# x in eight pieces, a first unit by halves, products of ones ahead of it, and transfers that wait for the landing two units back

## The chip, the core and the metric

The kernel runs on one core of a Trainium2 chip. The metric is the device time of one execution in microseconds (us). The engines that matter here: TensorE (PE in the profile, with PEld for its weight loads), VectorE (DVE), ScalarE (ACT) and the sync engine SP, which issues nearly all transfers from HBM. ACT can issue transfers too, on a queue of its own (ACTq in the profile; SP's is SPq). A semaphore orders work between engines: an instruction waits until a count is reached, and each engine works in program order, so what waits holds up all that stands behind it on its engine.

## The reference, cut to what matters

Two transformer blocks one after the other, on 256 tokens of 2048 features, in float32. Only the first step of the first block is touched here:

```
def first_block(x, mem, w_in, ...):
    h = rms_norm(x, g_mix[l])                       # x: [1, 256, 2048]
    qa, ka, va, qb, kb, vb, qc, kc, vc = jnp.split(h @ w_in[l], cuts, axis=-1)   # w_in: [2048, 6144]
    ... three attentions, w_out, cross attention, a gated feed-forward
def second_block(x, p, positions, ...):
    ... feed-forward, attention and recurrence, feed-forward, a gated output
```

What follows that first product reads the same numbers as before; some 600 MB of weights go through the chip once in all, and w_in is the first of them.

## The kernel before, in words

Activations lie transposed: features on the 128 partitions, in 16 chunks of 128 features, and 256 tokens along the free axis. x is X, 128 x 16 x 256.

Weights come in *units*: 256 rows by 512 columns (512 KB), as two chunks of 128 rows. Unit u lands in slot u % 4 of `raw`. Every float32 product is done as three products of a reduced-precision kind: a number is split into a high part and the rest. For a unit, ACT copies raw into `wh` with rounding (`split`, L1174), DVE subtracts and writes the rest into `wl` (`split`, L1761), and then PE multiplies high by high and rest, and rest by high (L675, L677, L680). The unit's counters are `raw_full` (landed), `hi_done`, `lo_done` and `units_used` (PE has read it). SP may load a unit into a slot when `lo_done` says that the unit four before it has been split, so from unit 4 on it waits there.

x takes the same two parts. For each chunk c ACT writes gain times x (L1314, counter `xs_hi`), and DVE the rest (L1989, `xs_lo`); the normalisation's factor, one over the root of the mean square, is multiplied in after the product, so the products can begin before it is known. PE needs xs_lo for the two chunks of unit u and lo_done for the unit.

The product with w_in goes by blocks of 512 columns, each of 8 units (8 x 2 chunks = all 2048 rows): units 0 to 7 are the first block, 8 to 15 the second. In the first block ACT and DVE prepare x beside the weights: two chunks of x, one unit, two chunks, one unit. Around it stands more:

- After unit 3 PE makes a small product for the position biases from three tables (L697, waits for `tab_loaded`). DVE adds to it, behind unit 7's split (L1995, `rt_sb`), and ACT stores the sum to HBM (L1317) before it goes on to unit 8.
- Then ACT takes turns between the splits of units 8 to 11 and the squares of x by four chunks (L1306); DVE takes turns between the rest of the splits and the sums of these squares (L1908, L1895, L1896). Between them DVE makes a small lambda (L2005 to L2008, from `lam`), and collects the first block's product (L1775) behind ACT's copy of it (L1192).
- PE sums the squares over partitions with a matrix of ones (`late_stat`, L634) at a fixed place in its order: after unit 10, the third of the second block. It waits there for `colsum_ready`, which DVE's L1896 sets.

At the program's start SP issues x in four pieces of four chunks (512 KB each), each ahead of one of units 0 to 3. ACT issues seven transfers of its own: all gain vectors (`vec`, 264 KB), a gate bias, the identity, the three tables and lambda's four vectors spread over all partitions. The first use of ACT's function table loads it (ACT_TABLE_LOAD).

Of the kernel before, what the change touches and what calls it, by code (L numbers as in the profile page):

```python
# [22 lines left out]
F32 = mybir.dt.float32  # L23
F32R = mybir.dt.float32r
I32 = mybir.dt.int32
ALU = mybir.AluOpType
ACT = mybir.ActivationFunctionType
AX_X = mybir.AxisListType.X

P = 128  # L30
# [176 lines left out]
def program(nc, a, out):  # L207
    with ExitStack() as ctx:
# [40 lines left out]
        def sem(name):  # L249
            return ctx.enter_context(nc.semaphore(name))  # L250
# [6 lines left out]
        x_in = [sem(f"x_in{i}") for i in range(4)]  # L257
# [208 lines left out]
        def _(sp):  # L466
            def load_x(g):
                sp.dma_start(X[:, 4 * g:4 * g + 4, :], a["x"].rearrange("(c p) t -> p c t", p=P)[:, 4 * g:4 * g + 4, :])\
                  .then_inc(x_in[g], 16)

# [8 lines left out]
            def stream(name, col, weight, rows=256, width=NB):  # L479
                ph = PH[name]  # L480

                def first_pair():

                    for u in range(2 * ph["upc"]):
                        src = weight(u % 2)[u // 2 * rows:(u // 2 + 1) * rows, bass.ds(col(u % 2, 0), width)]
                        load(ph["u0"] + u, 0, src.rearrange("(k p) n -> p k n", p=P))

                def block(c, i):
                    if name in PAIRED and isinstance(i, int) and c < 2:
                        if c == 0:  # L490
                            first_pair()
                        return
                    for u in range(ph["upc"]):
                        w, first = weight(c), col(c, i)
                        if name == "w_in" and c == 0 and u < 4:
                            load_x(u)
                        src = w[u * rows:(u + 1) * rows, bass.ds(first, width)]
                        load(ph["u0"] + c * ph["upc"] + u, i * (2 * ph["upc"]),
                             src.rearrange("(k p) n -> p k n", p=P))
                run_blocks(sp, ph, block, peel=1 if name == "w_in" or name in PAIRED else 0)  # L500
# [65 lines left out]
        def _(pe):  # L566
# [69 lines left out]
            def gemm(name, opr, ready, tiles=4, norm=None, after=None, cross=False, half=None, post=False):  # L636
# [9 lines left out]
                def block(c, i):  # L646
# [8 lines left out]
                    for v in range(2 * ph["upc"] if paired else ph["upc"]):  # L655
# [11 lines left out]
                        pe.wait_ge(lo_done, i * (2 * ph["upc"]) + (n + 1))  # L667
# [21 lines left out]
                        else:  # L689
                            for k in range(chunks):  # L690
                                if singly:
                                    pe.wait_ge(xs_lo, half + k + 1)
                                mm = chunk(k, range(tiles))
# [20 lines left out]
            gemm("w_in", *from_op(XS["mix"]), norm="mix")  # L714
# [443 lines left out]
        def _(act):  # L1158
            act.dma_start(vec[:, :], a["vec"]).then_inc(vec_loaded, 16)
            act.dma_start(SM[0:24, 56:57], a["gate_b"]).then_inc(gb_loaded, 16)  # L1160
            act.dma_start(ident[:, :], a["cst"][:, 0:P]).then_inc(cst_loaded, 16)
            act.dma_start(HF[0:32, 0:16], a["table"]).then_inc(tab_loaded, 16)
            act.dma_start(HF[0:32, 512:1024], a["onehot"]).then_inc(tab_loaded, 16)
            act.dma_start(HF[0:16, 1024:1536], a["diag"]).then_inc(tab_loaded, 16)
            act.dma_start(T2[:, 0, :], a["lam"].rearrange("a n -> (a n)").partition_broadcast(P))\
               .then_inc(lam_loaded, 16)
# [143 lines left out]
            for u in range(DC // 2):  # L1310
                if u % 2 == 0:
                    act.wait_ge(x_in[u // 2], 16)
                for c in (2 * u, 2 * u + 1):
                    act.activation(OPR[:, c, 0, :], X[:, c, :], ACT.Copy, scale=v("g_mix", c)).then_inc(xs_hi, 1)  # L1314
                split(u, 0)
# [434 lines left out]
        def _(dve):  # L1750
# [232 lines left out]
            dve.wait_ge(vec_loaded, 16)  # L1983
            for u in range(DC // 2):
                if u % 2 == 0:
                    dve.wait_ge(x_in[u // 2], 16)
# [4 lines left out]
                split(u, 0)  # L1991
# [751 lines left out]
```

## Time and profile before

| | us |
|---|---|
| median of 3 runs | 3259.98 (3259.1 to 3260.28) |
| profiled execution | 3258.8 |
| its span, first to last instruction | 3256.7 |
| PE busy in it | 3225.5 (99%) |
| DVE busy | 2100.2 (64%) |
| ACT busy | 1586.5 (49%) |
| first product of PE starts at | 10.09 |

The profiled execution is one run; its time is 2.1 us more than its span, and 1.2 us under the median of the runs. All times below are counted from the span's start. In a timeline the first number is an instruction's start and the second its length; lengths on PE overlap, so that what a product costs is read from start to start.

### The profile page before, as it was taken

Reading aid. Unit: us, or ns where it says so; the run is one execution under the profiler, and the core shown is the slowest. Engines: PE = TensorE matmul, PEld = TensorE weight load, DVE = VectorE, ACT = ScalarE, POOL = GpSimd, SP = SyncE. Lnnn points to the kernel's source line nnn. Section 1 sums busy time; section 2 is a strip of 40 time slices with the busy share of each in tenths; the row PEclk is TensorE's granted clock in tenths of the full one; section 3 lists DMA queues with packets and bytes.
Section 4 is the critical chain, followed back from the end, with each engine's and each line's share of the span. In section 5 each row is a group of like instructions: output and inputs, shape, how many; then the busy total and the mean of one; then the engine's idle time right before and its main releaser. Section 6 shows DMA issues by size and latency. Waiting matters only on the chain.

```text
span 3256.7 us, 51030 instructions
## 1 busy us (share of the span) xinstructions
PE 3225.5 (99%) x19828; PEld 2867.5 (88%) x19828; DVE 2100.2 (64%) x2266; ACT 1586.5 (49%) x1897; POOL 88.5 (3%) x36
## 2 busy tenths in 40 slices
PE   8999999999999999999999999999999999999997
PEld 7999988888888888888888888999988888888886
DVE  6666777766665556655555456867986656554568
ACT  5445555555454435544444344555744444444354
POOL 0000200000000100000000010000010000000101
PEclk9999999999999999999999999999999999999999
DMA  8555655666666565666565555654556565566654
GB/s 265 176 156 158 193 176 173 190 186 189 189 183 193 187 192 162 189 192 187 180 199 188 188 188 168 208 180 130 171 166 188 181 197 185 184 194 192 190 176 135
DMA packets 322172, 596.30 MB, mean 183 GB/s; under 512 B 18309, under 2 KB 42277, under 8 KB 322021
## 3 DMA queue, kind: packets, MB, share of 16 engines
q1 hardware_dynamic: 313872, 587.27, 58.7%
q10 hardware_dynamic: 8148, 6.90, 0.7%
q8 instruction: 109, 1.79, 0.2%
q14 instruction: 43, 0.34, 0.0%
HBM read 591.97 MB, written 2.13 MB: 182 GB/s over the span
## 4 chain that ended last, share of the span: by engine, by line
PE 96%; DVE 2%; ACT 1%; issue 0%; POOL 0%; DMA 0%; ACTq 0%; DVEq 0%; POOLq 0%
PE acc L675 26%; PE acc L677 25%; PE acc L680 24%; PE acc L728 5%; PE acc L731 5%; PE acc L730 5%; DVE WHL L1761 0%; PE acc L959 0%; PE acc L581 0%; PE acc L755 0%; PE acc L920 0%; PE acc L921 0%; PE acc L842 0%; PE acc L840 0%; PE acc L841 0%
## 5 line engine op out<-in xcount | busy, mean ns | idle before, releaser
L1761 DVE TENSOR_TENSOR WHL<-raw,WHL 128x1024 fp32r<-128x1024 f32 x1112 | 1384.7, 1256 | 977.0 <-ACT WHL L1174 975.9
L1174 ACT ACTIVATE WHL<-raw 128x1024 fp32r<-128x1024 f32 x1112 | 1164.3, 1057 | 1260.0 <-PE acc L680 1019.7
L677 PEld LDWEIGHTS acc<-OPR,WHL 128*128 128x128 f32 x4928 | 926.7, 188 | 204.1
L675 PE MATMUL acc<-OPR,WHL 128*128 128x512 f32 x2624 | 1026.0, 397 | 11.5 <-DVE WHL L1761 10.3
L677 PE MATMUL acc<-OPR,WHL 128*128 128x256 f32 x4928 | 996.6, 278 | 0.0
L680 PE MATMUL acc<-OPR,WHL 128*128 128x512 f32 x2304 | 911.7, 396 | 0.0
L675 PEld LDWEIGHTS acc<-OPR,WHL 128*128 128x128 f32 x2624 | 498.1, 190 | 29.9 <-issue 13.5
L677 PEld LDWEIGHTS acc<-HR,WHL 128*128 128x128 f32 x2184 | 410.3, 188 | 94.5
L675 PE MATMUL acc<-HR,WHL 128*128 128x512 f32 x1120 | 440.3, 395 | 0.0
L677 PE MATMUL acc<-HR,WHL 128*128 128x256 f32 x2184 | 433.9, 278 | 0.0
L680 PEld LDWEIGHTS acc<-OPR,WHL 128*128 128x128 f32 x2304 | 431.9, 187 | 0.0
L680 PE MATMUL acc<-HR,WHL 128*128 128x512 f32 x1064 | 420.9, 396 | 0.0
L728 PE MATMUL acc<-OPR,WHL 128*128 128x256 f32 x1216 | 349.5, 287 | 0.0
L731 PE MATMUL acc<-OPR,WHL 128*128 128x256 f32 x1216 | 343.9, 283 | 0.0
L730 PE MATMUL acc<-OPR,WHL 128*128 128x256 f32 x1216 | 343.9, 283 | 0.0
L728 PEld LDWEIGHTS acc<-OPR,WHL 128*128 128x128 f32 x1216 | 232.7, 191 | 5.4 <-issue 3.6
L730 PEld LDWEIGHTS acc<-OPR,WHL 128*128 128x128 f32 x1216 | 232.8, 191 | 1.6 <-issue 0.7
L731 PEld LDWEIGHTS acc<-OPR,WHL 128*128 128x128 f32 x1216 | 232.7, 191 | 0.0
L675 PEld LDWEIGHTS acc<-HR,WHL 128*128 128x128 f32 x1120 | 212.5, 190 | 2.6
L680 PEld LDWEIGHTS acc<-HR,WHL 128*128 128x128 f32 x1064 | 199.4, 187 | 0.0
L1192 ACT ACTIVATE T<-acc 128x1024 f32<-128x1024 f32 x91 | 92.0, 1011 | 18.2 <-PE acc L680 15.6
L1495 ACT ACTIVATE HR<-T 128x1024 f32 (+1 forms) x33 | 35.0, 1061 | 127.3 <-DVE T L2242 122.5
(374 smaller groups left out, 2093.7 us busy)
## 6 DMA issues: line engine op xcount, KB each, us to landing
raw<-in_w_up SPq DMA_DIRECT2D x176, 512.0 KB, 4.5
raw<-in_ff_w_gate SPq DMA_DIRECT2D x176, 512.0 KB, 3.8
raw<-in_ff_w_up SPq DMA_DIRECT2D x176, 512.0 KB, 4.4
raw<-in_ff_w_down SPq DMA_DIRECT2D x176, 512.0 KB, 4.1
raw<-in_w_in SPq DMA_DIRECT2D x170, 512.0 KB, 4.2
raw<-in_w_down SPq DMA_DIRECT2D x88, 512.0 KB, 4.3
raw<-in_w_out SPq DMA_DIRECT2D x64, 512.0 KB, 4.1
raw<-in_w_ple_gate SPq DMA_DIRECT2D x32, 512.0 KB, 4.9
```

The lines of the kernel that those rows point to most:

```text
L675: pe.matmul(acc[:, b + t, :], wh[:, s, col:col + P], x, start=first, stop=False)
L677: mm = pe.matmul(acc[:, b + t, 0:T], wl[:, s, col:col + P], x[:, 0, :], start=False, stop=last and t % 2 == 0)
L680: mm = pe.matmul(acc[:, b + t, :], wh[:, s, col:col + P], x, start=False, stop=last)
L728: pe.matmul(dst, w_hi, ks[k][:, 0, :], start=first and k == 0 and t % 2 == 0, stop=False, skip_group_check=True)
L730: pe.matmul(dst, w_hi, ks[k][:, 1, :], start=False, stop=False, skip_group_check=True)
L731: mm = pe.matmul(dst, w_lo, ks[k][:, 0, :], start=False, stop=last and k == 1, skip_group_check=True)
L1174: act.activation(wh[:, s, :], raw[:, s, :], ACT.Copy).then_inc(hi_done, 1)
L1192: act.activation(T1[:, 0:tiles, :], acc[:, b:b + tiles, T:2 * T], ACT.Copy).then_inc(t1_full, 1)
L1495: act.activation(HR[:, bass.ds(i * 4 + 4 * j, 4), 0, :], T2[:, :, :], ACT.Copy).then_inc(hid_hi, 1)
L1761: dve.tensor_tensor(wl[:, s, :], raw[:, s, :], wh[:, s, :].bitcast(F32), ALU.subtract)\
```

## The change

- x comes in eight pieces of two chunks (256 KB), one ahead of each of units 0 to 7.
- From unit 2 on SP issues x's piece and the unit only when the unit two back has landed (a wait on `raw_full`). The wait on `lo_done` from unit 4 on stays.
- Unit 0 comes as two transfers of 128 rows (256 KB each); ACT and DVE split each half by itself, between the chunks of x, and PE begins with the first half as soon as that and chunk 0 are there (`half=XS["mix"]` makes it wait for each chunk).
- ACT issues only the first 16 columns of `vec` (the gain of x, 8 KB). The three tables move to SP, between x's piece and unit 4; the rest of `vec`, the gate bias, the identity and lambda's vectors move to SP, between x's last piece and unit 7.
- ACT makes one copy of a single column at once, so that the function table is loaded there.
- PE makes 11 products of ones (128 x 128, float32) before the first unit.

```diff
             def load_x(g):
-                sp.dma_start(X[:, 4 * g:4 * g + 4, :], a["x"].rearrange("(c p) t -> p c t", p=P)[:, 4 * g:4 * g + 4, :])\
+                sp.dma_start(X[:, 2 * g:2 * g + 2, :], a["x"].rearrange("(c p) t -> p c t", p=P)[:, 2 * g:2 * g + 2, :])\
                   .then_inc(x_in[g], 16)
+
+            def load_tables():
+                sp.dma_start(HF[0:32, 0:16], a["table"]).then_inc(tab_loaded, 16)
+                sp.dma_start(HF[0:32, 512:1024], a["onehot"]).then_inc(tab_loaded, 16)
+                sp.dma_start(HF[0:16, 1024:1536], a["diag"]).then_inc(tab_loaded, 16)
+
+            def load_constants():
+                sp.dma_start(vec[:, 16:NVEC], a["vec"][:, 16:NVEC]).then_inc(vec_loaded, 16)
+                sp.dma_start(SM[0:24, 56:57], a["gate_b"]).then_inc(gb_loaded, 16)
+                sp.dma_start(ident[:, :], a["cst"][:, 0:P]).then_inc(cst_loaded, 16)
+                sp.dma_start(T2[:, 0, :], a["lam"].rearrange("a n -> (a n)").partition_broadcast(P))\
+                  .then_inc(lam_loaded, 16)
...
-                        if name == "w_in" and c == 0 and u < 4:
+                        if name == "w_in" and c == 0:
+                            if u >= 2:
+                                sp.wait_ge(raw_full[(u - 2) % SLOTS], 16 * ((u - 2) // SLOTS + 1))
                             load_x(u)
+                            if u == 4:
+                                load_tables()
+                            if u == 7:
+                                load_constants()
+                        if name == "w_in" and c == 0 and u == 0:
+                            sp.dma_start(raw[:, 0, 0:NB], w[0:P, 0:NB]).then_inc(w_first, 16)
+                            sp.dma_start(raw[:, 0, NB:2 * NB], w[P:2 * P, 0:NB]).then_inc(raw_full[0], 16)
+                            continue
...
-                        pe.wait_ge(lo_done, i * (2 * ph["upc"]) + (n + 1))
+                        if n > 0:
+                            pe.wait_ge(lo_done, i * (2 * ph["upc"]) + (n + 1))
...
+                                if n == 0 and k == 0:
+                                    pe.wait_ge(lo_first, 1)
+                                if n == 0 and k == 1:
+                                    pe.wait_ge(lo_done, 1)
...
-            gemm("w_in", *from_op(XS["mix"]), norm="mix")
+            pe.wait_ge(ones_set, 3)
+            for _ in range(11):
+                pe.matmul(acc[:, 7, 0:P], ones[:, :], ones[:, :], start=True, stop=True)
+            gemm("w_in", *from_op(XS["mix"]), half=XS["mix"], norm="mix")
...
-            act.dma_start(vec[:, :], a["vec"]).then_inc(vec_loaded, 16)
...
+            act.dma_start(vec[:, 0:16], a["vec"][:, 0:16]).then_inc(vec_loaded, 16)
+            act.wait_ge(ones_set, 1)
+            act.activation(SM[:, 62:63], SM[:, 60:61], ACT.Copy)
...
             for u in range(DC // 2):
-                if u % 2 == 0:
-                    act.wait_ge(x_in[u // 2], 16)
+                act.wait_ge(x_in[u], 16)
                 for c in (2 * u, 2 * u + 1):
                     act.activation(OPR[:, c, 0, :], X[:, c, :], ACT.Copy, scale=v("g_mix", c)).then_inc(xs_hi, 1)
-                split(u, 0)
+                    if c == 0:
+                        act.wait_ge(w_first, 16)
+                        act.activation(wh[:, 0, 0:NB], raw[:, 0, 0:NB], ACT.Copy).then_inc(hi_first, 1)
+                    if c == 1:
+                        act.wait_ge(raw_full[0], 16)
+                        act.activation(wh[:, 0, NB:2 * NB], raw[:, 0, NB:2 * NB], ACT.Copy).then_inc(hi_done, 1)
+                if u >= 1:
+                    split(u, 0)
+            act.wait_ge(vec_loaded, 32)
             act.wait_ge(rt_sb, 1)
...
+            def lo_half(k, full, done):
+
+                dve.wait_ge(full, 1)
+                part = slice(k * NB, (k + 1) * NB)
+                dve.tensor_tensor(wl[:, 0, part], raw[:, 0, part], wh[:, 0, part].bitcast(F32), ALU.subtract)\
+                   .then_inc(done, 1)
```

DVE's loop changes as ACT's does: `lo_half` behind chunk 0 and chunk 1, `split(u, 0)` from unit 1 on, and a wait for 32 on `vec_loaded` behind the loop.

The end of SP's start, before (the fourth piece of x and all that follows it; in brackets what a row waits for):

```order
L468 DMA X<-in_x 128x4x256
L477 DMA raw<-in_w_in 128x2x512
L468 DMA X<-in_x 128x4x256
L477 DMA raw<-in_w_in 128x2x512
L477 DMA raw<-in_w_in 128x2x512 [waits lo_done] x92
```

SP now, from x's third piece to the end of the first block (`raw_full0` to `raw_full3` are the landings of units 0 to 3, and of units 4 and 5 when they are waited for again; T_58 holds lambda's vectors):

```order
L469 DMA X<-in_x 128x2x256 [waits raw_full2]
L473 DMA HF<-in_table 32x16
L474 DMA HF<-in_onehot 32x512
L475 DMA HF<-in_diag 16x512
L490 DMA raw<-in_w_in 128x2x512 [waits lo_done]
```

```order
L469 DMA X<-in_x 128x2x256 [waits raw_full1]
L478 DMA vec<-in_vec 128x513
L479 DMA SM<-in_gate_b 24x1
L480 DMA ident<-in_cst 128x128
L481 DMA T_58<-in_lam 128x256
L490 DMA raw<-in_w_in 128x2x512 [waits lo_done] x89
```

The first of the two is unit 4 with its piece of x, the second unit 7 (and the first row of all later units): three and four transfers stand ahead of these units now, behind a wait for units 2 and 5, where before all pieces of x went out without a wait.

ACT at its start, before, from its last own transfer on:

```order
L1165 DMA T_58<-in_lam 128x256
L1314 ACT_TABLE_LOAD [waits x_in0]
L1314 ACTIVATE OPR<-X,vec 128x256 [waits vec_loaded]
L1314 ACTIVATE OPR<-X,vec 128x256
L1174 ACTIVATE WHL<-raw 128x1024 [waits raw_full0]
```

and now:

```order
L1190 DMA vec<-in_vec 128x16
L1192 ACT_TABLE_LOAD
L1192 ACTIVATE SM<-SM 128x1 [waits ones_set]
L1339 ACTIVATE OPR<-X,vec 128x256 [waits x_in0,vec_loaded]
L1342 ACTIVATE WHL<-raw 128x512 [waits w_first]
L1339 ACTIVATE OPR<-X,vec 128x256
L1345 ACTIVATE WHL<-raw 128x512 [waits raw_full0]
```

The table's load no longer stands behind a wait for x, and the first half of unit 0 stands behind one chunk of x instead of the whole unit behind two. From unit 8 on the rows of ACT, DVE and PE are the same in both kernels, in the same order.

## Rows read from the trace of the kernel before

**Rows 1.** The page: the chain that ended last, by engine.
```profile
PE 96%; DVE 2%; ACT 1%; issue 0%; POOL 0%; DMA 0%; ACTq 0%; DVEq 0%; POOLq 0%
```

**Rows 2.** The chain of waits, first 60 us: start, length, what.
```profile
0.75 4.71 DMA X<-in_x
5.54 1.28 ACT L1314
6.83 0.91 ACT OPR L1314 x2
7.74 0.95 ACT WHL L1174
8.72 1.24 DVE WHL L1761
```

**Rows 3.** Timeline of PE: start, length, line, operation; in brackets idle before.
```profile
10.09 0.77 PE L675 MATMUL acc<-OPR,WHL 128*128 128x512 f32 x1 [10.09 <-DVE WHL L1761]
10.87 0.63 PE L675 MATMUL acc<-OPR,WHL 128*128 128x512 f32 x1
...
14.51 0.47 PE L675 MATMUL acc<-OPR,WHL 128*128 128x512 f32 x1
...
24.17 0.50 PE L675 MATMUL acc<-OPR,WHL 128*128 128x512 f32 x1
...
35.42 0.39 PE L675 MATMUL acc<-OPR,WHL 128*128 128x512 f32 x1
...
43.81 0.59 PE L634 MATMUL acc<-S,ones 128*128 128x256 f32 x2
...
3239.16 1.99 PE L612 MATMUL acc<-S,ones 128*128 128x256 f32 x8 [0.75 <-ACT S L1228]
```

**Rows 4.** DMA in four stretches: the last number is GB/s.
```profile
0.00:4.20 4.20, 0.00 (x0) 0.00 (x0) 0.26 (x3) 0.00 (x0) 0.20 (x4) 1.00 0.43 130
0.00:5.45 5.45, 0.00 (x0) 0.00 (x0) 0.26 (x3) 0.00 (x0) 0.20 (x4) 1.00 0.58 189
0.00:7.60 7.60, 0.00 (x0) 0.00 (x0) 0.38 (x4) 2.05 (x3) 0.20 (x4) 1.00 0.73 240
12.00:20.00 8.00, 7.97 (x43) 6.70 (x42) 5.17 (x7) 5.95 (x10) 0.00 (x0) 1.00 1.06 381
```

**Rows 5.** Timeline of DVE: the ones, units 6 and 7, and the sums of squares.
```profile
0.91 0.17 DVE L1982 MEMSET ones<- 128x128 f32 x1
...
24.66 1.22 DVE L1761 TENSOR_TENSOR WHL<-raw,WHL 128x1024 fp32r<-128x1024 f32 x1
...
26.59 1.22 DVE L1761 TENSOR_TENSOR WHL<-raw,WHL 128x1024 fp32r<-128x1024 f32 x1
...
42.27 0.69 DVE L1895 TENSOR_TENSOR S<-S 128x512 f32<-128x512 f32 x1
43.00 0.42 DVE L1896 TENSOR_TENSOR S<-S 128x256 f32<-128x256 f32 x1
```

**Rows 6.** Timeline of ACT, the splits of units 8 and 11.
```profile
28.84 1.06 ACT L1174 ACTIVATE WHL<-raw 128x1024 fp32r<-128x1024 f32 x1 [3.02 <-DVE HF L1995]
...
35.68 1.06 ACT L1174 ACTIVATE WHL<-raw 128x1024 fp32r<-128x1024 f32 x1 [0.78 <-PE acc L680]
```

**Rows 7.** Timelines of SP and ACT: transfers issued, start and length.
```profile
1.25 0.50 SPq L477 DMA_DIRECT2D raw<-in_w_in  x1
...
2.40 0.95 ACTq L1162 DMA_DIRECT2D HF<-in_table  x1
...
4.61 0.54 ACTq L1165 DMA_DIRECT2D T<-in_lam  x1
...
31.19 0.37 SPq L477 DMA_DIRECT2D raw<-in_w_in  x1
```

**Rows 8.** Issue to landing, units issued at 31.19 and 35.48, each alone.
```profile
raw<-in_w_in SPq DMA_DIRECT2D x1, 512.0 KB, 3.6
...
raw<-in_w_in SPq DMA_DIRECT2D x1, 512.0 KB, 4.8
```

More of the change, by code:

```diff
@@ L256, in program @@
         hid_hi, hid_lo = sem("hid_hi"), sem("hid_lo")
-        x_in = [sem(f"x_in{i}") for i in range(4)]
+        x_in = [sem(f"x_in{i}") for i in range(8)]
+        w_first, hi_first, lo_first = sem("w_first"), sem("hi_first"), sem("lo_first")
         out_stored, vec_loaded, cst_loaded = sem("out_stored"), sem("vec_loaded"), sem("cst_loaded")
@@ L1158, in _ @@
         def _(act):
-            act.dma_start(vec[:, :], a["vec"]).then_inc(vec_loaded, 16)
[L1160 to L1166, printed above, removed]
+            act.dma_start(vec[:, 0:16], a["vec"][:, 0:16]).then_inc(vec_loaded, 16)
+            act.wait_ge(ones_set, 1)
+            act.activation(SM[:, 62:63], SM[:, 60:61], ACT.Copy)
             def split(u, i, upc=0):
@@ L1983, in _ @@
             dve.wait_ge(vec_loaded, 16)
+            def lo_half(k, full, done):
[3 more added lines that the diff above has]
+                   .then_inc(done, 1)
             for u in range(DC // 2):
-                if u % 2 == 0:
-                    dve.wait_ge(x_in[u // 2], 16)
+                dve.wait_ge(x_in[u], 16)
                 for c in (2 * u, 2 * u + 1):
@@ L1990, in _ @@
                                              ALU.mult, ALU.subtract).then_inc(xs_lo, 1)
-                split(u, 0)
+                    if c == 0:
+                        lo_half(0, hi_first, lo_first)
+                    if c == 1:
+                        lo_half(1, hi_done, lo_done)
+                if u >= 1:
+                    split(u, 0)
+            dve.wait_ge(vec_loaded, 32)
             dve.wait_ge(rt_ps, 1)
```

## The prediction

> **What bounds the kernel now.** I read the page's chain first: PE is 96% of it [rows 1], so time can be won or lost only where PE does not yet work or has to wait. The edits touch the first 45 us or so, and there the chain of waits names a single long stretch without PE: x's first piece lands at 5.46, ACT loads its table (1.28), rounds two chunks of x (0.91), splits the unit (0.95), DVE writes the rest (1.24) [rows 2], and PE's first product starts at 10.09 [rows 3]. From there PE runs without a gap that matters. So the first question is how much of the 10.09 us goes; the second, which the rest of this text decides on, is who is late next.
>
> For that I followed the timelines of PE, DVE and ACT to the first place where PE meets their results in a fixed order: the sum of squares (L634), at 43.81 [rows 3]. DVE sets its input at 43.00 + 0.42 = 43.42 [rows 5]. That is 0.39 us before PE comes. Before, nobody waits there, but if PE comes more than 0.39 us earlier and DVE does not, PE waits.
>
> **PE's start.** A landing can be read in bytes: when x's first piece landed, 189 GB/s x 5.45 us = 1.03 MB had moved [rows 4], of which x and the gain vectors, first in their queues, were 0.795; so 0.235 MB of later transfers went with them. Now the order is x's piece 0, two halves of unit 0, x's piece 1 (0.262 MB each) and unit 1 (0.524). With the same curve of bytes, piece 0 needs 0.27 + 0.235 = 0.505 MB, there at about 4.2 (130 x 4.2 = 0.546), the first half 0.767 MB at 4.8, the second at 5.45, piece 1 at 6.2, unit 1 at 1.816 MB, 7.6 (240 x 7.6 = 1.82) [rows 4]. Then:
>
> - the table's load (1.28 [rows 2]) is no longer behind x: ACT does it while it waits anyway; it would cost part of this again only if x landed before some 2.5 (start, one issue and the load);
> - ACT: one chunk 0.45 (half of the 0.91), to 4.65; the first half at 4.8, 0.62 long (between 0.45 for 256 columns and 0.95 for 1024 [rows 2]), to 5.4;
> - DVE: the rest of the half, 0.69 (a 128x512 operation [rows 5]), to 6.15, and PE 0.13 later, as before (8.72 + 1.24 to 10.09 [rows 2, 3]): 6.3.
>
> Bounds: 5.6 if piece 0 lands at 3.5, 7.6 if it lands as late as x's first piece did.
>
> **The first unit's pace.** Unit 0 took 14.51 - 10.09 = 4.42 us, a later one (35.42 - 24.17) / 4 = 2.81 [rows 3]: the first product of the unit lasts 0.77 and one soon after 0.63, one at 35.42 only 0.39. The products of ones, 11 of float32, cost some 0.25 each at the upper level (8 instructions of 256 columns in 1.99 [rows 3]), twice that at the lower: 2.7 to 5.5 us from about 1.1 on, when DVE has set the ones [rows 5], so that they end between 3.8 and 6.6, and at worst delay the first unit by 0.3. I take the 1.6 as won: unit 0 ends at 9.1. If not, it ends at 10.7; the sum below shows that it makes no difference.
>
> **Unit 1 and PE's arrival.** Unit 1 lands at 7.6; ACT 1.06 [rows 6], DVE 1.23, the two hand-overs and PE's 0.13 make 10.1, so PE waits about a microsecond for it. Before it began at 14.51, and 29.3 us after that PE came to L634 [rows 3]. If all landings keep up, PE now comes there at 10.1 + 29.3 = 39.4: 4.4 us earlier. That is the gain if nothing else is late.
>
> **Who is late: SP's queue.** DVE's sums need ACT's squares, and these come in ACT's order behind the store of the bias sums, which waits for DVE's addition, which stands behind unit 7's split on DVE. So everything there hangs on the landing of unit 7. Before, SP had no wait ahead of the pieces of x, and DVE split the units at its own pace (24.66 to 26.59, 1.93 us a unit [rows 5]). Now SP's order holds x's piece and unit u until unit u - 2 is there, and behind the wait stand three transfers ahead of unit 4, four ahead of unit 7, and all later units.
>
> Prices. With two units in flight, a unit and its piece of x are 0.786 MB, at 381 GB/s [rows 4] 2.06 us apart. A unit issued alone landed after 3.6 us, another after 4.8 [rows 8]; I take 3.6, since it also includes no other traffic, and keep 4.8. An issue took 0.50 on SP in the start and 0.37 later; three of the moved ones took 4.61 - 2.40 = 2.21 on ACT while SP issued too, 0.74 each [rows 7]. Alone on SP they should lie between 0.42 and 0.74; I take 0.58.
>
> - Unit 0 lands at 5.45, unit 1 at 7.6, unit 2 at 9.65, unit 3 at 11.7.
> - Piece 4 goes out at 9.7, the tables until 9.7 + 0.5 + 3 x 0.58 = 11.95, unit 4 then, landing at 15.55. Unit 5 follows at 17.6.
> - Unit 6 waits for unit 4, unit 7 for unit 5: piece 7 at 17.65, four constants, unit 7 at 17.65 + 0.5 + 2.33 = 20.5, landing at 24.1.
>
> PE needs none of these sooner: units 2 to 7 have to be there some 2.4 us (ACT's split, DVE's and the hand-over) before PE comes, at 12.9, 15.7, 19.5 (behind the tables' product: 24.17 - 14.51 less three units, 1.2 [rows 3]), 22.3, 25.1 and 27.9, and they are.
>
> From unit 7's landing ACT's split and hand-overs take 1.15, and from the start of DVE's split to ACT's split of unit 8 it took 28.84 - 26.59 = 2.25 [rows 5, 6]: unit 8 is split from 27.5 on. From there to the sum's end it took 43.42 - 28.84 = 14.58 [rows 5, 6], of which DVE lost some 0.26 to ACT's wait for PE at unit 11 (0.78 [rows 6]); PE is ahead now, so 14.3. The sum is there at 27.5 + 14.3 = 41.8, and PE goes on at 41.9.
>
> The sum: 43.81 - 41.9 = **1.9 us** won. PE waits from 39.4 to 41.9, which swallows 2.5 of the 4.4, and also whatever the start and the clock's pace do better or worse by less than 2.5. Behind L634 the order is the old one and all engines stand to each other as before, so the shift stays. Against the profiled execution, 3258.8 - 1.9 = 3256.9 (span 3254.8); against the median, 3259.98 - 1.9 = **3258.1**.
>
> A rule on the landing: the Trainium skill, "DMA: Bandwidth & Descriptors", section "Anatomy of one DMA", gives a transfer some 2.0 us and its bytes over 436 GB/s, fitted on another issuing path; an estimate from it is 3.2 us for a unit, less than either row shows. By that units 4 and 7 would each be 0.4 sooner and the time 3257.3.
>
> Range of this case: with 0.42 an issue unit 7 lands at 22.8 and the gain is 3.2; with 0.74, at 25.2 and 0.8.
>
> **The rivals.**
>
> - *PE is not held at L634.* If unit 7 lands by 21.6 (issues of 0.37 and landings quicker than 3.6, or DVE's part after unit 8 shorter than I read), PE's own arrival decides: 4.4 us, 3255.6; with PE's start at 5.6 and no wait at unit 1, up to 6: 3254. For it: 381 GB/s leaves room. Against: two waits in series, each behind a full landing.
> - *SP's waits are longer than what they free: slower.* Place: SP, ahead of unit 7. From unit 7's landing at 26.0 on the gain is nothing. With 4.8 us from issue to landing instead of 3.6 for every unit issued behind a wait, units 2 to 5 land at 10.8, 13.0, 17.95 and 20.0, unit 7 is issued at 22.9 and lands at 27.7; PE goes on at 45.5, 1.7 later: 3261.7. For it: the 4.8 of rows 8. Against: it was one of two, and both engines that follow have slack.
> - *PE falls back to 1.2 GHz while it waits 2.5 us at L634.* No row has such a gap: the longest I can show is 0.75, behind which 8 instructions took 1.99 us, the upper level's pace [rows 3]. If it falls, the start's 1.6 us is the price: 3259.7. The Trainium skill, "TensorE: Matmul & The Clock Gate", section "HAM oscillation", says that gaps in PE's work put the array back to half its clock; no run here shows it for a gap of this length.
> - *The change doesn't start PE earlier*, since x's first bytes come no sooner: PE at 7.6, L634 reached at 40.7. That is still before 41.9: the same time.
>
> **How the numbers follow.** Held at L634 (with the last rival in it) 0.58; PE's own arrival 0.22; slower through SP 0.13; fallen clock 0.07. A measurement here can tell about 0.2%, 6.5 us, from no change. The first case's own range is 3256.8 to 3259.2, and with both unknowns, issue and landing, up to 3260. The range I give, 3254.8 to 3260.8, holds that, most of the second case, the fourth, and leaves out the second's upper end and most of the third: some 0.2. Faster by over 0.2% would need 3253.5, beyond the second case's best: 0.04. Slower by over 0.2% needs unit 7 later than 32: 0.03. Within: 0.93.
>
> **What would show it.** In the new profile: PE's products of ones from about 1.1, its first product of the unit near 6.3 at lengths near 0.4; a wait of about 1 us at unit 1; unit 7 issued near 20.5 and landing near 24; ACT's split of unit 8 near 27.5; and in PE's waits an idle time of 2 to 3 us at the sum of squares, put down to DVE's last fold. If PE has no wait there, the second case is true; if the sum comes after 43.8, the third. Products of 0.6 us behind the wait would be the fourth.

## The result and the profile after

The changed kernel takes 3263.67 us (median of 21 runs, 3262.15 to 3265.48), the kernel before 3259.10 on the same chip (21 runs, 3258.7 to 3260.28): ratio 1.0014 with a 95% interval of 1.0008 to 1.0019, that is 4.6 us slower (2.6 to 6.2). By the bound of 0.2% that is no change; by its sign it is the other way, and the forecast of 3258.1 and its range (to 3260.8) both miss. The profiled execution took 3264.77 us (span 3262.8).

All lines of the code moved: the unit's products are now L699 (before L675), the sum of squares L657 (L634), ACT's split L1200 (L1174), DVE's L1794 (L1761), the fold that sets the sum L1929 (L1896).

The page's chain by engine, which answers to [rows 1]:

```profile
PE 94%; DVE 3%; DMA 1%; ACT 1%; issue 1%; POOL 0%; SPq 0%; ACTq 0%; DVEq 0%; POOLq 0%
```

PE has 94% where it had 96, DVE, DMA and "issue" a point more each: PE waits for somebody that it did not wait for. The timeline of PE, against [rows 3], says where:

```profile
1.13 5.07 PE L744 MATMUL acc<-ones 128*128 128x128 f32 x22 [1.13 <-DVE ones L2015]
5.93 0.77 PE L699 MATMUL acc<-OPR,WHL 128*128 128x512 f32 x1
...
7.35 0.40 PE L699 MATMUL acc<-OPR,WHL 128*128 128x512 f32 x1
...
10.76 0.47 PE L699 MATMUL acc<-OPR,WHL 128*128 128x512 f32 x1 [1.14 <-DVE WHL L1794]
...
31.50 0.76 PE L699 MATMUL acc<-OPR,WHL 128*128 128x512 f32 x1 [2.60 <-DVE WHL L1794]
32.06 0.63 PE L701 MATMUL acc<-OPR,WHL 128*128 128x256 f32 x2
...
34.89 0.40 PE L704 MATMUL acc<-OPR,WHL 128*128 128x512 f32 x1
...
46.93 0.67 PE L657 MATMUL acc<-S,ones 128*128 128x256 f32 x2 [2.56 <-issue]
...
48.13 0.47 PE L699 MATMUL acc<-OPR,WHL 128*128 128x512 f32 x1
48.40 0.63 PE L701 MATMUL acc<-OPR,WHL 128*128 128x256 f32 x2
...
51.78 0.40 PE L699 MATMUL acc<-OPR,WHL 128*128 128x512 f32 x1
...
135.71 0.71 PE L786 MATMUL acc<-HF,T 64*128 64x256 f32 x4
```

Here is the larger part of the story. PE starts 4.2 us earlier than before (5.93 against 10.09) and waits for unit 1 as forecast. Then it waits 2.60 us for unit 7, which the forecast had in good time, and 2.56 us more at the sum of squares, where it goes on at 46.93: 3.1 us later than before's 43.81 (it had come there at 44.37, itself late by unit 7's wait and the slow products behind that). From 48.40 to 51.7 the products last 0.63 us instead of 0.40 and stand 0.43 apart instead of 0.23, which costs 1.6 us more. So at the first product of the attention PE is 4.7 us behind before, whose row was

```profile
130.98 0.71 PE L755 MATMUL acc<-HF,T 64*128 64x256 f32 x4
```

and 4.7 us is close to the difference of the medians (4.6). The two profiled executions differ by more, 6.0 us at the end, and that comes later: the same instructions are 4.7 us behind at 300 us, 5.1 from 400 to 2000 us, and 6.0 from 2200 us on. The step near 370 us (0.4) is in all profiles of kernels made from the changed one, and not in that of the kernel before with the waits alone; these runs do not show what makes it.

Who is late? ACT's splits, against [rows 6]; the three are units 4, 7 and 8:

```profile
17.41 1.06 ACT L1200 ACTIVATE WHL<-raw 128x1024 fp32r<-128x1024 f32 x1 [2.85 <-DMA raw<-in_w_in]
...
29.04 1.06 ACT L1200 ACTIVATE WHL<-raw 128x1024 fp32r<-128x1024 f32 x1 [5.27 <-DMA raw<-in_w_in]
...
32.48 1.06 ACT L1200 ACTIVATE WHL<-raw 128x1024 fp32r<-128x1024 f32 x1 [2.38 <-DVE HF L2040]
```

Unit 8's split has gone from 28.84 to 32.48, because unit 7 landed only at 29.0. DVE follows at the old distance. Its fold, against [rows 5]:

```profile
46.40 0.42 DVE L1929 TENSOR_TENSOR S<-S 128x256 f32<-128x256 f32 x1
```

32.48 to 46.82 is 14.3 us, the forecast's figure. It holds beyond this kernel: in all ten profiles in which PE waits for the sum, PE begins it 14.4 to 14.5 us after ACT begins unit 8's split. PE's wait is named "issue", but it ends 0.11 us after this fold. The chain of waits, against [rows 2], has the two long links on the way there:

```profile
12.18 5.21 DMA raw<-in_w_in
...
21.62 7.40 DMA raw<-in_w_in
```

Unit 4, issued at 12.18 behind the three tables, took 5.2 us to land, unit 7, issued at 21.62 behind the four constants, 7.4; both were forecast with 3.6. SP's issues, against [rows 7]:

```profile
17.40 0.37 SPq L469 DMA_DIRECT2D X<-in_x  x1
...
19.34 0.37 SPq L469 DMA_DIRECT2D X<-in_x  x1
19.75 0.47 SPq L478 DMA_DIRECT2D vec<-in_vec  x1
20.26 0.45 SPq L479 DMA_DIRECT2D SM<-in_gate_b  x1
20.76 0.35 SPq L480 DMA_DIRECT2D ident<-in_cst  x1
21.15 0.43 SPq L481 DMA_DIRECT2D T<-in_lam  x1
```

Both pieces of x wait until the unit two back is there (17.40 and 19.34: units 4 and 5). The issues themselves are cheap, 2.28 us from x's last piece to unit 7. What the transfers do meanwhile is in the windows, against [rows 4] (the columns are the same: length, five engines, granted clock, share of the DMA engines, GB/s):

```profile
12.00:20.00 8.00, 8.00 (x45) 6.28 (x43) 4.96 (x8) 4.63 (x8) 0.00 (x0) 1.00 0.81 257
18.00:19.00 1.00, 1.00 (x8) 0.87 (x7) 0.50 (x1) 1.00 (x3) 0.00 (x0) 1.00 0.40 100
21.00:22.50 1.50, 1.50 (x11) 1.28 (x10) 1.46 (x3) 0.80 (x2) 0.00 (x0) 1.00 0.97 336
23.00:23.50 0.50, 0.50 (x4) 0.41 (x4) 0.49 (x1) 0.50 (x2) 0.00 (x0) 1.00 0.25 48
24.50:25.00 0.50, 0.50 (x4) 0.41 (x4) 0.50 (x2) 0.00 (x0) 0.00 (x0) 1.00 0.86 168
27.00:29.00 2.00, 1.91 (x12) 1.41 (x10) 0.00 (x0) 0.00 (x0) 0.00 (x0) 1.00 1.05 404
32.00:34.00 2.00, 2.00 (x8) 1.74 (x7) 0.43 (x1) 1.52 (x2) 0.00 (x0) 0.50 0.71 199
48.00:50.00 2.00, 2.00 (x9) 1.68 (x8) 1.82 (x2) 2.00 (x3) 0.00 (x0) 0.58 0.38 68
```

From 12 to 20 the engines moved 257 GB/s where before they moved 381. From 18 to 19, while SP waits, they stand at 100. From 22.5 to 25, when the constants are due, 333 packets of together 0.28 MB go by, at rates of 46 to 184, and only near the end do the engines move in full again, at 404 GB/s for units 7, 8 and 9; SP issued the last two right behind unit 7. (The filled wait, below, starts in the same way up to the sum and repeats this: unit 7 issued at 21.34, landed at 28.8.) The last two rows show the granted clock behind PE's two waits: half of the 2.4 GHz, over all of one stretch and most of the other.

### The profile page after: what moved, and what is told of

The parts are those of the page before. It is cut to its first block, busy times and chain, and to the rows that moved or that the text cites. A ratio compares the mean times of both kernels' runs of the same rounds, so it can differ in the third digit from the quotient of the medians.

```text
span 3262.8 us, 51089 instructions
## 1 busy us (share of the span) xinstructions
PE 3233.5 (99%) x19850; PEld 2874.1 (88%) x19850; DVE 2103.3 (64%) x2267; ACT 1587.6 (49%) x1899; POOL 88.4 (3%) x36
## 4 chain that ended last, share of the span: by engine, by line
PE 94%; DVE 3%; DMA 1%; ACT 1%; issue 1%; POOL 0%; SPq 0%; ACTq 0%; DVEq 0%; POOLq 0%
PE acc L699 26%; PE acc L701 25%; PE acc L704 23%; PE acc L759 5%; PE acc L762 5%; PE acc L761 5%; DVE WHL L1794 1%; DMA raw<-in_w_in 1%; ACT WHL L1200 0%; PE acc L604 0%; DMA raw<-in_cmp_k_w 0%; PE acc L786 0%; PE acc L951 0%; PE acc L952 0%; PE acc L873 0%
## 5 line engine op out<-in xcount | busy, mean ns | idle before, releaser
L1794 DVE TENSOR_TENSOR WHL<-raw,WHL 128x1024 fp32r<-128x1024 f32 x1111 | 1387.8, 1260 | 982.2 <-ACT WHL L1200 981.0
L1200 ACT ACTIVATE WHL<-raw 128x1024 fp32r<-128x1024 f32 x1111 | 1163.4, 1057 | 1266.4 <-PE acc L704 1018.6
L699 PE MATMUL acc<-OPR,WHL 128*128 128x512 f32 x2624 | 1026.6, 397 | 5.1 <-DVE WHL L1794 3.9
L699 PEld LDWEIGHTS acc<-OPR,WHL 128*128 128x128 f32 x2624 | 498.6, 190 | 23.5 <-issue 6.5
L699 PE MATMUL acc<-HR,WHL 128*128 128x512 f32 x1120 | 440.3, 395 | 0.0
L699 PEld LDWEIGHTS acc<-HR,WHL 128*128 128x128 f32 x1120 | 212.5, 190 | 2.6
```

What stands on the lines that cost most here:

```text
L699: pe.matmul(acc[:, b + t, :], wh[:, s, col:col + P], x, start=first, stop=False)
L1200: act.activation(wh[:, s, :], raw[:, s, :], ACT.Copy).then_inc(hi_done, 1)
L1794: dve.tensor_tensor(wl[:, s, :], raw[:, s, :], wh[:, s, :].bitcast(F32), ALU.subtract)\
```

## The experiments

Each was timed against the kernel before on the same chip (31 or 33 runs of it, median 3259.3 to 3259.8; beside the changed kernel it was 3259.1). The medians of before thus differ by up to 0.7 us, and the 95% intervals of the ratios are about 3 us to either side: a difference of a microsecond or less between two rows of the table is not shown by their medians. The sum of squares is L636 to L661 in them. In the table, unit 7 and the sum are from the profiled execution; the medians are over 10 or 11 runs, 21 for the changed kernel.

| | unit 7 issued, landed | PE at the sum [wait] | median us | ratio to before |
|---|---|---|---|---|
| changed kernel | 21.62, 29.0 | 46.93 [2.56] | 3263.67 | 1.0014 [1.0008, 1.0019] |
| no landing waits | 16.20, 23.5 | 42.14 [0] | 3257.37 | 0.9995 [0.9986, 1.0004] |
| constants late | 18.80, 24.2 | 42.09 [2.25] | 3258.45 | 0.9998 [0.9989, 1.0007] |
| both | 15.94, 22.3 | 42.12 [0] | 3257.60 | 0.9992 [0.9983, 1.0001] |
| waits at units 2 and 3 alone, constants late | 15.95, 22.4 | 40.34 [0.36] | 3256.62 | 0.9991 [0.9982, 1.0000] |
| ... without the ones | 15.81, 23.2 | 41.09 [0.66] | 3256.65 | 0.9990 [0.9981, 1.0000] |
| before + waits | 18.82, ≤ 23.7 | 44.17 [0] | 3258.54 | 0.9996 [0.9987, 1.0005] |
| lambda from other rows | 20.55, 26.5 | 44.39 [3.40] | 3262.66 | 1.0010 [1.0001, 1.0020] |
| lambda late | 22.75, 28.4 | 46.28 [3.36] | 3262.80 | 1.0010 [1.0001, 1.0019] |
| gains late | 20.88, 27.8 | 45.72 [3.45] | 3263.25 | 1.0012 [1.0003, 1.0022] |
| three small ones late | 19.30, 26.1 | 44.02 [3.36] | 3261.72 | 1.0006 [0.9996, 1.0015] |
| followers held | 20.50, 26.4 | 44.73 [3.36] | 3262.81 | 1.0011 [1.0001, 1.0021] |
| wait filled | 21.34, 28.8 | 46.68 | 3263.20 | 1.0012 [1.0003, 1.0021] |

**The landing waits taken out** (e4):

```diff
-                            if u >= 2:
-                                sp.wait_ge(raw_full[(u - 2) % SLOTS], 16 * ((u - 2) // SLOTS + 1))
```

> The changed kernel without SP's waits for the landing two units back; the constants stay ahead of unit 7, lambda's among them. Unit 7 then waits only for unit 3's split (DVE ends it at 15.0 in the changed kernel). Theory A: unit 7 still takes 6 to 8 us from issue to landing, but is issued near 15 to 17 and lands at 22 to 24; PE does not wait there, the sum of squares comes at 40 to 42, time 3256 to 3258. Theory B expects the same or better, 3256, but with 4 us from issue to landing. If the waits protect the first units as they are meant to, PE's first product or unit 1 comes later than 5.9 and 10.8.

Unit 7 goes out 5.4 us earlier and lands 5.5 earlier. The loss is gone: 6.3 us below the changed kernel. DMA while the constants' packets go by, what unit 7 took from issue to landing, and PE at the sum:

```profile
18.00:20.00 2.00, 2.00 (x13) 1.77 (x12) 1.91 (x4) 1.87 (x3) 0.00 (x0) 1.00 1.07 363
```

```profile
raw<-in_w_in SPq DMA_DIRECT2D x1, 512.0 KB, 7.3
```

```profile
42.14 0.59 PE L655 MATMUL acc<-S,ones 128*128 128x256 f32 x2
```

The 7.3 us are a warning on reading landings: with units and pieces ahead in a queue that never runs dry, a long way from issue to landing costs nothing, since the issue is early by as much. PE comes to the sum itself, without a wait, but not as early as it might: without the waits unit 1 is late, PE begins it at 11.44 after a wait of 2.11 us, and the granted clock is 0.50 from 13 to 15 us. That is what the waits at the first units are good for.

**The four constants behind unit 11, all waits kept** (e3):

```diff
-                            if u == 7:
-                                load_constants()
+                        if name == "w_in" and c == 1 and u == 4:
+                            load_constants()
```

> The changed kernel, SP's waits kept, with all four constants (rest of the gains, gate bias, identity, lambda) issued behind unit 11 instead of ahead of unit 7; ACT and DVE wait for the gains' rest only behind the squares. Theory D (the small transfers ahead of unit 7, all four together, hold it back, whichever of them): unit 7 is issued at about 19.8 and lands at about 23.8 (4 us), unit 8 is split from about 27.3, the sum of squares comes at about 41.7, PE waits there 1 to 2 us; time about 3257.5. Theory B (the waits on landings alone are too slow): unit 7 still lands after 26, time 3260 or more.

This, too, takes the loss away by itself: 5.2 us. Unit 7's and unit 8's splits and PE at the sum:

```profile
24.18 1.06 ACT L1200 ACTIVATE WHL<-raw 128x1024 fp32r<-128x1024 f32 x1 [0.39 <-DMA raw<-in_w_in]
27.57 1.06 ACT L1200 ACTIVATE WHL<-raw 128x1024 fp32r<-128x1024 f32 x1 [2.33 <-DVE HF L2039]
```

```profile
42.09 0.67 PE L657 MATMUL acc<-S,ones 128*128 128x256 f32 x2 [2.25 <-issue]
...
42.82 0.40 PE L701 MATMUL acc<-OPR,WHL 128*128 128x256 f32 x2
```

From the landing on these rows are the prediction's own path to two tenths (24.1, 27.5, PE on at 41.9). The landing itself agrees by two differences that cancel: issued at 18.80, since no constants stand ahead, it took 5.4 us, with units 8 and 9 behind it. The products behind the wait are at 0.40.

**Both** (e7), the last two edits together:

```diff
-                            if u >= 2:
-                                sp.wait_ge(raw_full[(u - 2) % SLOTS], 16 * ((u - 2) // SLOTS + 1))
...
-                            if u == 7:
-                                load_constants()
+                        if name == "w_in" and c == 1 and u == 4:
+                            load_constants()
```

> The changed kernel without SP's landing waits and with all four constants behind unit 11. Without the waits alone the time was 3257.4 and PE reached the sum of squares without a wait, 1.7 us earlier than in the kernel before, since unit 1 was late (PE began it at 11.4). So both theories expect no more than that here: 3257 to 3257.5, unit 7 landing by 21 to 22. Lower only if something other than PE's arrival held that run.

3257.60, within 0.9 us of either edit alone. So the four combinations are 3263.7 (waits and constants), 3258.45 (waits alone), 3257.37 (constants alone), 3257.60 (neither): neither costs anything that can be told by itself; together they cost 5 to 6 us. That is an interaction, not a sum, and it is there in unit 7's landing already, before any slack of PE: 29.0, 24.2, 23.5 and 22.3.

**The waits in the kernel before** (e9): x in eight pieces and the same waits, with the constants and tables on ACT's queue as before.

```diff
+                            if u >= 2:
+                                sp.wait_ge(raw_full[(u - 2) % SLOTS], 16 * ((u - 2) // SLOTS + 1))
                             load_x(u)
```

> The kernel before, with x in eight pieces and SP's landing waits, and nothing else: constants and tables on ACT's queue as before, unit 0 whole, no products of ones. Theory B: the waits by themselves make it slower, unit 7 lands after 26 and the sum of squares comes after 44; time 3261 or more. Theory D: without the small transfers in SP's order the waits cost nothing, unit 7 lands at 21 to 24; PE starts near 8 to 9.5; 3257.5 to 3259.

No cost: PE reaches the sum at 44.17 without a wait, and the time is that of before. From 12 to 20 us the DMA engines moved 342 GB/s, against 381 in the kernel before and 257 in the changed one. Two units in flight feed PE well enough as long as nothing else stands in that queue.

**Lambda's transfer.** It reads one row of 1 KB into all 128 partitions. First the same bytes from 128 different rows (e1):

```diff
-                sp.dma_start(T2[:, 0, :], a["lam"].rearrange("a n -> (a n)").partition_broadcast(P))\
+                sp.dma_start(T2[:, 0, :], a["x"][0:P, :])\
```

> The changed kernel, but the transfer of lambda's vectors (one row of 1 KB read 128 times) is replaced by one of the same size from 128 different rows of x (so lambda is wrong). In the changed kernel it was issued at 21.15 and took 6.3 us, and unit 7, issued right behind it at 21.62, took 7.4 us and landed at 29.0. Theory A (reading one row 128 times is slow, and unit 7 stands behind it in the same queue): unit 7 lands 4 to 4.5 us after its issue, at about 25.8; ACT's split of unit 8 moves from 32.5 to about 29.3, the sum of squares from 46.9 to about 43.7, PE hardly waits at unit 7, and the time falls by 3 to 5 us to about 3259.5. Theory B (it is not that transfer: unit 7 is late since SP may issue it only behind landings): unit 7 still lands near 29, time 3263.7. Theory C (only the clock that falls in PE's waits costs time): landings as in B.

Then lambda behind unit 11 (e2; `load_lam` is its transfer, taken out of `load_constants`):

```diff
+                        if name == "w_in" and c == 1 and u == 4:
+                            load_lam()
```

> The changed kernel, with lambda's transfer alone issued behind unit 11 instead of ahead of unit 7; DVE needs it only after unit 11's split. Theory A: unit 7 is issued about 0.5 earlier, near 21.1, lands near 25, unit 8 is split from about 28.5, the sum of squares comes near 43 and the time is about 3258.5, a little under the kernel before. Theory B: unit 7 lands near 28.5, and the time is about 3263.

From other rows lambda's transfer lands after 5.0 us instead of 6.3 and unit 7 after 5.9 instead of 7.4, but the time falls by only 1.0; taken away altogether, by 0.9. Lambda is at most a part and not the cause. The part cannot be sized from one profile each: a kernel with lambda in its old form (followers held, below) shows 5.1 and 5.9, too. The packets in the traces do not settle it: lambda's 128 packets of 1 KB ran from 23.0 to 27.1 us in the changed kernel, with unit 7 behind them, 0.14 us each in the mean, and from other rows it was 0.08; but in the old form it was also 0.08 (gains late), 0.06 (followers held) and 0.05 (no landing waits).

**The gains of the later norms late** (e10), 257 KB, and **the other three late** (e11):

```diff
-                sp.dma_start(vec[:, 16:NVEC], a["vec"][:, 16:NVEC]).then_inc(vec_loaded, 16)
...
+                        if name == "w_in" and c == 1 and u == 4:
+                            sp.dma_start(vec[:, 16:NVEC], a["vec"][:, 16:NVEC]).then_inc(vec_loaded, 16)
```

> The changed kernel with the rest of the gains (256 KB) alone issued behind unit 11; gate bias, identity and lambda stay ahead of unit 7, SP's waits stay. With all four late unit 7 landed 5.4 us after its issue (24.2); with all four ahead 7.4 (29.0). If the bytes ahead of it count, the gains are most of them (0.26 of 0.46 MB): unit 7 lands at 25 to 26, the sum comes near 43.5, about 3260. If the small ones with their short pieces count, unit 7 still lands at 27.5 or later, 3262.5.

```diff
-                sp.dma_start(SM[0:24, 56:57], a["gate_b"]).then_inc(gb_loaded, 16)
...
+                        if name == "w_in" and c == 1 and u == 4:
+                            load_small()
```

> The complement: gate bias, identity and lambda behind unit 11, the rest of the gains ahead of unit 7. If bytes count, unit 7 lands at 26 to 27.5, about 3262; if the small ones count, at 24.5 to 25.5, 3259 to 3260, near the run with all four late.

The gains gave back 0.4 us, the three small ones 2.0, all four 5.2: again more than their sum, though the first is not told apart from nothing. Measured by the expectations, the first run speaks for the small ones (unit 7 lands at 27.8) and the second for the bytes (at 26.1), so neither theory holds alone. None of the four can be named as the cause; what each leaves is still late enough for PE's wait. A late sum is also not all that they lose: with the three small ones late the sum comes only 0.2 us after before's, but the granted clock is 0.50 behind it, and at 60 us the same instructions are 1.6 behind.

**Units 8 and later held until unit 7 has landed** (e13):

```diff
+                        if name == "w_in" and c == 1 and u == 0:
+                            sp.wait_ge(raw_full[3], 32)
```

> The changed kernel with one more wait on SP: units 8 and later are issued only when unit 7 has landed (before, units 8 and 9 went out within 1.5 us behind it). If a transfer's landing is held up by what is issued behind it (a unit alone landed after 3.6 us in the kernel before), unit 7 lands 5 to 6 us after its issue instead of 7.4, at about 27, the sum comes about 2 us sooner, and the time is about 3261.5. If only what stands ahead counts, unit 7 lands as before near 29 and the time is 3263.7 or a little more, since units 8 and 9 come later.

Unit 7's landing, and the DMA engines up to it:

```profile
raw<-in_w_in SPq DMA_DIRECT2D x1, 512.0 KB, 5.9
```

```profile
21.00:22.00 1.00, 1.00 (x8) 0.91 (x7) 0.55 (x2) 1.00 (x2) 0.00 (x0) 1.00 0.69 176
22.00:23.00 1.00, 1.00 (x7) 0.85 (x6) 1.00 (x2) 0.56 (x2) 0.00 (x0) 1.00 0.69 170
23.00:24.00 1.00, 1.00 (x8) 0.89 (x7) 0.81 (x3) 0.00 (x0) 0.00 (x0) 1.00 0.91 322
24.00:25.00 1.00, 1.00 (x7) 0.87 (x7) 0.00 (x0) 0.00 (x0) 0.00 (x0) 1.00 0.36 127
25.00:26.50 1.50, 1.50 (x10) 1.28 (x9) 0.00 (x0) 0.06 (x1) 0.00 (x0) 1.00 0.05 19
```

Unit 7 lands 1.5 us sooner after its issue, unit 8, issued late now, makes ACT wait 2.8 us where it waited 2.4 for DVE, and the time falls by only 0.9. (The profiled execution is a fast one, 3261.17 against a median of 3262.81.) The slow stretch (176 and 170 GB/s) is there without any follower beside it, so units 8 and 9 do not make it; and the last row shows that even an undisturbed landing comes over a microsecond after nearly all bytes have moved.

**PE's wait at the sum filled with ten more products of ones** (e5):

```diff
+                if ph["name"] == "w_in":
+                    for _ in range(10):
+                        pe.matmul(acc[:, 7, 0:P], ones[:, :], ones[:, :], start=True, stop=True)
```

> The changed kernel with 10 more products of ones on PE, in its wait for the sum of squares (behind the wait for the first block's collection, which ends near 44.5; the sum comes at 46.9). PE's order behind it is the same. Theory C in part (the products behind the wait run at 1.2 GHz from 48.3 to 51.6, some 1.6 us lost): they now last 0.4 us from the start and the time is 1 to 2 us less, about 3262. If the clock costs nothing in the end, 3263.7.

```profile
44.34 2.50 PE L657 MATMUL acc<-ones 128*128 128x128 f32 x20
46.68 0.68 PE L660 MATMUL acc<-S,ones 128*128 128x256 f32 x2
47.01 0.58 PE L702 MATMUL acc<-OPR,WHL 128*128 128x512 f32 x1
47.42 0.40 PE L704 MATMUL acc<-OPR,WHL 128*128 128x256 f32 x2
```

The sum is as late as in the changed kernel (46.68), the products behind it stay at 0.40, and the profiled span is 1.7 us shorter (3261.1 against 3262.8). The median gains only 0.5, not told apart from nothing. So the slow stretch behind the sum is a price of the wait and not of the change's other parts, 1.6 us in the profile. Of the other kernels with a long wait there, four paid it in their profiles (lambda from other rows, lambda late, gains late, three small ones late: 1.4 to 1.6 us) and one did not (followers held); how many of the unprofiled executions pay it, these runs leave open.

**The best version** (e8): the constants late, and landing waits for units 2 and 3 only.

```diff
-                            if u >= 2:
+                            if u in (2, 3):
```

> The changed kernel with SP's landing waits at units 2 and 3 alone and all four constants behind unit 11. Unit 1 is as early as in the changed kernel (PE begins it at 10.3 to 10.8) and from unit 4 on SP waits for DVE only. Theory: unit 7 lands by 22, the sum of squares is there at 40 or before, PE arrives at about 40 and hardly waits; about 4 us under the kernel before, 3255 to 3256. If unit 7 still lands after 24, the tables or x's pieces cost as much as the waits.

```profile
22.43 1.06 ACT L1200 ACTIVATE WHL<-raw 128x1024 fp32r<-128x1024 f32 x1 [0.24 <-DMA raw<-in_w_in]
```

```profile
40.34 0.67 PE L657 MATMUL acc<-S,ones 128*128 128x256 f32 x2 [0.36 <-issue]
...
127.58 0.71 PE L786 MATMUL acc<-HF,T 64*128 64x256 f32 x4
```

PE is at the sum 3.5 us earlier than before and 3.4 earlier at the attention (127.58 against 130.98); the median is 3.1 us below before and 7 below the changed kernel. This is what PE's earlier start is worth at the sum; as a time it is not quite shown, since the interval reaches 1. In the profiled execution 1.2 of the 3.4 us are left at the end (span 3255.5 against 3256.7): 0.4 goes near 370 us, as in all these kernels, and most of the rest between 2060 and 2150 us, where PE is idle 1.9 us in all instead of 0.25. Against the kernel with all waits and the constants late, PE is 1.75 us earlier at the sum (40.34 for 42.09): from unit 4 on the waits do cost a part of the gain.

**The same without the products of ones** (e12):

```diff
-            pe.wait_ge(ones_set, 3)
-            for _ in range(11):
-                pe.matmul(acc[:, 7, 0:P], ones[:, :], ones[:, :], start=True, stop=True)
```

> The version with landing waits at units 2 and 3 alone and all constants late (3256.6), without the 11 products of ones. There PE waited only 0.4 at the sum of squares, so what PE loses at the start should now count, unless its wait at unit 1 (1.3 us) takes it: at 1.2 GHz unit 0 takes about 4.4 instead of 3.1, so unit 1 begins no later than now or 0.3 later, but if the array also falls back in that wait, its products lose more. 3256.6 to 3258.5; in the changed kernel itself the products would cost or save nothing.

```profile
5.99 0.77 PE L699 MATMUL acc<-OPR,WHL 128*128 128x512 f32 x1 [5.99 <-DVE WHL L2018]
...
9.97 0.63 PE L699 MATMUL acc<-OPR,WHL 128*128 128x512 f32 x1
...
10.82 0.40 PE L704 MATMUL acc<-OPR,WHL 128*128 128x512 f32 x1
```

The first unit now runs at 0.63 us a product, and the time is the same, 3256.65. With the ones PE waited 1.30 us for unit 1; without them it doesn't wait there. Of the 1.6 us that they win, 1.3 are a wait for the next unit; PE comes to the sum 0.45 us later without them (40.43 for 39.98) and still waits there.

## Why the prediction was wrong

*Right: the start.* PE's first product came at 5.93 (6.3 forecast), at the level of 0.40 from 7.35 on; unit 1 at 10.76 (10.1), with the wait forecast there.

*Right: who decides.* PE is held at the sum of squares, unit 7's landing sets it over unit 8's split, 3.4 us from landing to that split (29.0 to 32.48; forecast 24.1 to 27.5) and 14.3 from the split to the sum. In e3, where the landing came out as forecast, the rest of this path did, too.

*Wrong: the price of a landing.* "A unit issued alone landed after 3.6 us, another after 4.8 [rows 8]; I take 3.6, since it also includes no other traffic, and keep 4.8." Both of these rows are of a unit alone. For units 2, 3 and 6 of the changed kernel, with no small transfer ahead, it came near (3.8, 4.0 and 4.1). Units 4 and 7 were to be issued behind three and four small transfers in the same queue, and unit 7 ahead of units 8 and 9. They took 5.2 and 7.4. Of the 4.9 us that unit 7 was late (29.0 for 24.1), 1.1 came through its issue (21.62 for 20.5: unit 5 landed at 19.35 instead of 17.6, since unit 4 was late, and the issues, 2.28 for 2.83, gave 0.55 back) and 3.8 through its landing (7.4 for 3.6). What makes up the landing can be read from four cases, one profile each: about 4.0 with neither constants ahead nor units 8 and 9 behind (units 2, 3 and 6), 5.4 with the two units behind alone (e3), 5.9 with the constants ahead alone (e13), 7.4 with both. So the constants take some 1.9 us of it, and the units behind 1.4, as far as single profiles tell. The rate agrees roughly: from 22.5 to 27.0 the engines moved 0.83 MB; at 381 GB/s it would have been 1.7, an estimate of 2.3 us lost in the slow stretch.

*Wrong: the rate.* "381 GB/s leaves room" was read where nothing waited [rows 4]. In the changed kernel the same stretch ran at 257, with 100 in one microsecond (18 to 19), while unit 6 had only just been let go by unit 4's landing. The waits alone do not do that: with them in the kernel before (e9) it was 342. (One profile each: in e3, whose order of transfers is the same up to there, it was 291.) With the small transfers in the same queue a unit is late, the next issue waits for it, and the small ones come when there is little beside them to fill the engines (a share of 0.25 from 23.0 to 23.5). In e4 they go by beside the units, and the rate stays at 363.

*The rival that came true* was the third, at the place that it named (SP ahead of unit 7), and past the landing at 26.0 from which it was to decide. It had a chance of 0.13, and with 4.8 us a landing still came out at 3261.7, with unit 7 at 27.7. It is not the waits alone, as its name said: e9 and e3 have them at no cost against the kernel before. It is the waits and what was put behind them.

*The clock* was given 0.07 as a case of its own and came on top of the late sum, at the 1.6 us that it was priced with. Of the 4.7 us at 130 us, 3.1 are the late sum and 1.6 the products behind it.

*That PE does not start earlier* and *that it is not held at the sum* were both wrong for this kernel; the second is what e4 and e7 show.

*Not exact: "so the shift stays".* It stays to 300 us (4.7), but the profiles of all kernels made from the changed one lose 0.4 us more near 370 us, and the changed kernel's another 0.9 by 2200 us.

Open is why the four constants are moved so slowly. That lambda reads one row 128 times may account for some of it (e1), the gains for little, and not all pairs and threes of the four were tried. What the three tables cost ahead of unit 4 was not tried either: they stand there in every kernel made from the changed one.

## What to carry to other kernels

A transfer's price from issue to landing holds for the queue in which it was read: before small transfers are moved ahead of a large one behind a wait, look for a row in which they stand together, and otherwise take a range up to twice the price. A wait for a landing and small transfers in the same queue can each cost nothing and together cost what the change was to win, so put the small ones where no deadline follows. And an engine that gets ahead by 4 us wins only what its next fixed meeting point lets through.

## What the runs showed of the hardware

- While four transfers of together 460 KB (gains, gate bias, identity, lambda) went by ahead of unit 7, the DMA engines moved 46 to 248 GB/s from 22.5 to 26 us, in steps of half a microsecond, with shares of 0.25 to 0.97. Beside units, in a full queue, the rate was 363 (e4). With units and pieces of x it was 381 in the kernel before, with units alone 404.
- A unit's landing was 3.6 and 4.8 us after its issue alone, 5.2 behind three small transfers, 5.4 ahead of two units, 5.9 behind four small transfers, 7.4 behind four and ahead of two units, and 7.3 at no cost in a queue that was full.
- The lower level of the clock (0.50 granted) behind a wait of PE is not sure. It came behind 2.60 us and 2.56 (changed kernel), 2.11 (e4, at unit 1), 2.57 (e7, at unit 1), 2.49 (e5, at unit 7), and 3.36 to 3.45 at the sum in e1, e2, e10 and e11. Behind 2.25 (e3) and 3.36 (e13), both at the sum, it did not. In the changed kernel the products are slow from 31.50 to 34.6 and from 48.40 to 51.7; behind the sum that began only 1.5 us after the work did (46.93).
- The kernels in which PE waits for long spread more from run to run: 3.3 us in the changed kernel, 2.6 to 4.9 in the five with a wait of 3.4 us at the sum, 1.6 to 1.8 in the kernel before and in the best version.
